# A two-layer decoder trunk on one core: modulation vectors by multiply-and-sum on VectorE instead of reductions on TensorE, layer-norm sums in column groups, and two small moves of TensorE's steps

## The chip, the cores and the metric

One NeuronCore of a Trainium2 chip (trn2) runs the whole program. The metric is the device time of one execution in microseconds (us); the median over several executions counts. All tensors are float32; "fp32r" in a row is the one-pass form of float32 on TensorE, for which every operand is split beforehand into a high and a low part.

## What is computed

From the reference, for depth 2, sequence 512 and D = 1024:

```python
e = silu(c @ cond_w + cond_b)
for i in range(2):
    mod = (e @ ada_w[i] + ada_b[i]).reshape(B, 3, 3, D)
    shift, scale, gate = mod[:, :, 0], mod[:, :, 1], 1 + mod[:, :, 2]
    h = modulate(x, norm_g[i, 0], shift[:, 0], scale[:, 0])
    x = x + 0.5 * gate[:, 0] * swiglu(h, ffn_w1[i, 0], ffn_w3[i, 0], ffn_w2[i, 0])
    h = modulate(x, norm_g[i, 1], shift[:, 1], scale[:, 1])
    x = x + gate[:, 1] * mixer(h)          # i = 0: causal conv module, i = 1: stick-breaking attention
    h = modulate(x, norm_g[i, 2], shift[:, 2], scale[:, 2])
    x = x + 0.5 * gate[:, 2] * swiglu(h, ffn_w1[i, 1], ffn_w3[i, 1], ffn_w2[i, 1])
# modulate(x, g, shift, scale) = rms_norm(x, g) * (1 + scale) + shift
# the conv module: glu(h @ w_in) -> depthwise conv of width 31 -> silu(layer_norm) -> @ w_out
```

## The kernel before

The kernel is written by hand, engine by engine, in raw instructions with semaphores; every engine runs its list in order. x lies transposed in the on-chip memory, 8 chunks of 128 channels by 512 tokens. There are four feed-forward parts (`ffn(j, ...)`, j = 0 to 3), the convolution module between j = 0 and 1 and the attention between j = 2 and 3.

**Slabs.** Weights come as slabs from HBM: up slabs of 128x2048 (22 per feed-forward part), down slabs of 128x1408 (16 per part). SyncE (SP) loads each into `raw[n % 2]`, ScalarE (ACT) writes its high part (`hi`, L630; in an up step L696), VectorE (DVE) its low part (`lo`, L896; in an up step L1103), and TensorE (PE) multiplies with three matmuls per product: high by high, high by low, low by high (`triple`, L1491 to L1493). An up slab is 48 matmuls of 128x512. The semaphore `lo_done` lets PE start a slab, and `slab_done` tells that it is finished. An up step of DVE (`up_step`) multiplies by SiLU's result (L1095), writes the low part of the activations (L1099), then the slab's low part (L1103).

**Modulation.** The 9216 values per layer are computed in groups of 512 (`q`; 38 groups in all, of which the first two are `cond_w`). Groups 0 to 5 are done on PE at the start (`start_group`, L1638, stages `stage[...]`). The other 32 are woven into the feed-forward parts 0 to 2: SP loads half a group (1 MB) into `ada_raw` (`load_ada`), DVE forms a weighted sum in eight instructions of 128x512 per group (`ada_half`, L905 and L908), PE sums it over the partitions in `ada_reduce` (L1619, four column groups of 32), which stands in the middle of an up slab (`at_k`) or behind a down slab, and DVE turns the row into columns and adds the bias (`ada_take`, L920, L922). `Q_FFN`, `Q_BODIES` and `Q_DOWN` say in which step which group is done.

**Norms.** For each modulated norm (number m; m = 2 is the layer norm) PE sums the squares in the first slab (`sums`, L1593), DVE computes the factor (`factor`) and writes it as two diagonals `fac_hi` and `fac_lo` (L964), and PE spreads these over the partitions (`spread`, L1611 and L1613) ahead of chunk 5 of the first slab, followed by `bias_sums` (L1571). Behind it `h_lows` on DVE and `h_his` on ACT make the modulated h, for which the second slab waits chunk by chunk (L1512, L1519).

**Layer norm (m = 2).** The mean is spread by L1747 and L1749; `token_sums` (L1716) forms per-token sums with 128-column weights and one moving column, four blocks per sum, for the sum and the sum of squares of v; earlier, `pivot` does the same for the first chunks (L1723, L1716). DVE centres the chunks (`centre`, L929), computes the factor (and writes it as diagonals, L970), PE spreads it, and then chunk by chunk DVE multiplies (L1304), ACT applies SiLU and writes `h_hi` (L784, L787), DVE writes `h_lo` (L1310), and PE does the first slab of the output projection.

**The start.** The groups' weights come in first. PE does groups 0 and 1 (the vector e), then group 2 (scale's first half), eight matmuls that keep PE busy (L1696), three chunks of the first slab, group 3 (scale's second half), and the other chunks; ACT makes the input's high parts (L659) and DVE the low parts (L995).

Of the kernel before, what the change touches and what calls it, by code (L numbers as in the profile page):

```python
# [22 lines left out]
ALU = mybir.AluOpType  # L23
# [63 lines left out]
Q_FFN = [6, 20, 31]  # L87
Q_BODIES = [11, 11, 7, 0]
Q_DOWN = 17
# [8 lines left out]
def trunk(nc, x_in, up_in, down_in, mix_in, ada_in, vec_in, dw_in, dwb_in, con_in, ind_in, sel_in, out):  # L98
    ctx = ExitStack()
    with ctx:  # L100
# [103 lines left out]
        ada_ps = ps[:, 7, 0:8]  # L204
        ada_rows = ps[:, 7, 0:P].rearrange("p (n r) -> p n r", n=4)
# [3 lines left out]
        ln_sq, ln_sum = ps[:, 4, 0:4], ps[:, 0, 0:4]  # L209
        pivot_ps = ps[:, 7, 0:4]  # L210
# [19 lines left out]
        ada_sum = sem("ada_sum")  # L230
        mod_done = sem("mod_done")
# [6 lines left out]
        lnsum_done = sem("lnsum_done")  # L238
        off_step = sem("off_step")
# [164 lines left out]
        def _(sp):  # L404
# [18 lines left out]

            def ffn_loads(j):
                nb = Q_BODIES[j]
                with sp.Fori(0, min(nb, 10)) if nb else ExitStack() as i:
                    if nb:
                        up_loads(j, i, True)
                if nb < 10:
                    with sp.Fori(nb, 10) as i:  # L430
                        up_loads(j, i, False)
                for s in range(2):
                    load(N_DOWN[j] + s, down_in[2 * KD * j + s, :, :], DOWN)
                    if nb == 11:
                        load_ada(2 * (Q_FFN[j] + 10) + s)
                for lo_i, hi_i in ((1, 2), (2, KD)) if j == 0 else ((1, KD),):
                    with sp.Fori(lo_i, hi_i) as i:
                        for s in range(2):
                            sp.wait_ge(lo_done, N_DOWN[j] + 2 * i - 1 + s)
                            sp.dma_start(raw[s][:, 0:DOWN], down_in[2 * KD * j + 2 * i + s, :, :]) \  # L440
                                .then_inc(raw_s[s], 16)
                        if j == 0 and lo_i == 2:
                            load_ada(2 * Q_DOWN - 2 + i)

# [24 lines left out]

            for c in range(2):  # L470
                load(N_CONV + c, mix_in[c, :, :])
# [152 lines left out]
        def _(act):  # L624
# [19 lines left out]
            def root(m):  # L644
                if m == 2:
                    act.wait_ge(vec_step, 4 * m + 1)
                    act.activation(st[:, 4:8], st[:, 0:4], ACT.Sqrt).then_inc(sqrt_done, 1)
                    return
                act.wait_ge(stat_col, stat_cols(m))
                act.activation(st[:, 4:8], row_cols, ACT.Sqrt, bias=eps_col, scale=1.0 / D) \  # L650
                    .then_inc(sqrt_done, 1)
# [80 lines left out]
            hi(N_UP[0])  # L732
            table()
# [158 lines left out]
        def _(dve):  # L892
# [6 lines left out]
            def ada_half(q, s, buf, acc):  # L899

                for k in range(4):
                    a = 8 * q + (STEP0 - 48) + 4 * s + k
                    w = e_col[:, 4 * s + k:4 * s + k + 1]
                    if s == 0 and k == 0:
                        dve.tensor_scalar(acc, buf[:, k, :], w, None, ALU.mult).then_inc(ada_step, 1)  # L905
                    else:
                        dve.wait_ge(ada_step, a)
                        dve.scalar_tensor_tensor(out=acc, in0=buf[:, k, :], scalar=w, in1=acc, op0=ALU.mult,  # L908
                                                 op1=ALU.add).then_inc(ada_step, 1)
# [22 lines left out]
            def factor(m):  # L932

                vv, sd, y0, y1 = st[:, 0:4], st[:, 4:8], st[:, 8:12], st[:, 16:20]
                if m == 2:
                    dve.wait_ge(stat_done, m + 1)
                    dve.wait_ge(off_step, 3)
                    dve.scalar_tensor_tensor(out=vv, in0=ln_sq, scalar=1.0 / D, in1=off_sq, op0=ALU.mult,
                                             op1=ALU.subtract).then_inc(vec_step, 1)
                    centre(2)  # L940
# [18 lines left out]
                for part in range(2):  # L959
# [3 lines left out]
                    if m != 2:  # L963
                        dve.tensor_tensor(  # L964
                            (fac_hi, fac_lo)[part].rearrange("p (b c i) -> p b c i", b=4, c=4),
                            ident[:, :].rearrange("p (b c i) -> p b c i", b=4, c=1).broadcast_to((P, 4, 4, 32)),
                            (f32(st_r[:, :]), y0)[part].rearrange("p (b c i) -> p b c i", b=1, i=1).broadcast_to((P, 4, 4, 32)),
                            ALU.mult).then_inc(rdiag_done, 1)
                        continue
                    dve.tensor_tensor(  # L970
                        (fac_hi, fac_lo)[part].rearrange("p (c m) -> p c m", c=4),
                        ident[:, :].rearrange("p (c m) -> p c m", c=1).broadcast_to((P, 4, P)),
# [1008 lines left out]
```

## Time and profile before

| | |
|---|---|
| three runs | 1976.23, 1976.68 and 1977.87 us; median 1976.68 us |
| the profiled execution | 1978.21 us, span 1976.4 us (1.8 us lie around it) |
| PE busy | 1945.8 us, 98% |
| DVE busy | 1110.3 us, 56% |
| ACT busy | 661.9 us, 33% |
| mean granted TensorE clock | 0.997 |
| HBM | 252 MB read, 129 GB/s over the span |

Busy time of PE is the union of its matmuls, whose ends are modelled. How much a step of PE costs is better read from the distance of matmul starts. The instruction count of a group with 32-bit float operands on PE that are not fp32r is twice the number of calls, since each call is two passes.

### The profile page before, as it was taken

The page shows a single profiled execution, that of the slowest core. Times are in us where ns is not written, and L with a number is a line of the kernel's source. Part 1 is how long each engine was busy: PE and PEld are TensorE (multiplying, and loading weights), DVE is VectorE, ACT ScalarE, POOL GpSimd, SP SyncE. Part 2 cuts the span into 40 slices and gives each one's busy share as a digit, 9 for nine tenths or more (in the row PEclk, how much of TensorE's full clock was granted, in tenths as well). Part 3 has the DMA queues.
Part 4 walks back from the last instruction along what each step waited for, and adds up shares of the span by engine and source line. Part 5 has one row for each costly group of instructions (what it writes and reads, how often), then busy time and mean ns, then how long its engine had stood idle before and what let it go on. Part 6 is the DMA issues. An engine that isn't in the chain of part 4 may idle for free.

```text
span 1976.4 us, 24087 instructions
## 1 busy us (share of the span) xinstructions
PE 1945.8 (98%) x9444; PEld 1562.6 (79%) x9444; DVE 1110.3 (56%) x1351; ACT 661.9 (33%) x742; POOL 150.5 (8%) x101
## 2 busy tenths in 40 slices
PE   6999999999989999999999999999999999999999
PEld 5788888876577888888888888888778788888887
DVE  4865564589888565633666533246569774333222
ACT  3422222242254322222432222234248743222211
POOL 0100000121411000001100000111022020000000
PEclk9999999999989999999999999999999999999999
DMA  9454544436413545432354522323245323222232
GB/s 394 170 206 176 206 165 166 158 106 180 126 55 138 208 174 194 175 124 93 116 213 170 191 93 79 102 100 124 95 99 137 107 86 107 85 106 85 88 98 90
DMA packets 50777, 275.88 MB, mean 140 GB/s; under 512 B 7456, under 2 KB 8096, under 8 KB 25760
## 3 DMA queue, kind: packets, MB, share of 16 engines
q1 hardware_dynamic: 47648, 270.87, 39.0%
q10 hardware_dynamic: 3072, 4.23, 0.9%
q8 instruction: 37, 0.61, 0.1%
q14 instruction: 20, 0.16, 0.0%
HBM read 251.94 MB, written 2.10 MB: 129 GB/s over the span
## 4 chain that ended last, share of the span: by engine, by line
PE 89%; DVE 4%; ACT 2%; issue 1%; DMA 0%; ACTq 0%; DVEq 0%; SPq 0%
PE ps L1491 27%; PE ps L1493 26%; PE ps L1492 26%; PE ps L1734 2%; PE ps L1512 1%; PE ps L1837 1%; PE ps L1853 1%; PE ps L1823 1%; PE ps L1619 1%; PE ps L1519 1%; DVE w L896 0%; PE ps L1532 0%; PE ps L1537 0%; PE ps L1531 0%; ACT h_hi L676 0%
## 5 line engine op out<-in xcount | busy, mean ns | idle before, releaser
L1491 PE MATMUL ps<-h_hi,w 128*128 128x512 f32 x1552 | 610.5, 393 | 1.2 <-DVE h_lo L995 1.0
L1493 PE MATMUL ps<-h_hi,w 128*128 128x512 f32 x1552 | 605.0, 390 | 0.0
L1492 PE MATMUL ps<-h_lo,w 128*128 128x512 f32 x1552 | 604.8, 390 | 0.0
L1491 PEld LDWEIGHTS ps<-h_hi,w 128*128 128x128 f32 x1552 | 291.7, 188 | 74.2 <-issue 12.8
L1493 PEld LDWEIGHTS ps<-h_hi,w 128*128 128x128 f32 x1552 | 291.5, 188 | 61.2
L1492 PEld LDWEIGHTS ps<-h_lo,w 128*128 128x128 f32 x1552 | 291.8, 188 | 58.8
L896 DVE TENSOR_TENSOR w<-raw,w 128x1408 fp32r<-128x1408 f32 (+1 forms) x104 | 201.0, 1933 | 204.4 <-ACT w L630 204.4
L630 ACT ACTIVATE w<-raw 128x1408 fp32r<-128x1408 f32 (+1 forms) x104 | 164.7, 1583 | 418.0 <-PE ps L1493 405.8
L1491 PE MATMUL ps<-g_hi,w 128*128 128x512 f32 x704 | 274.5, 390 | 0.0
L1493 PE MATMUL ps<-g_hi,w 128*128 128x512 f32 x704 | 274.2, 389 | 0.0
L1492 PE MATMUL ps<-g_lo,w 128*128 128x512 f32 x704 | 274.2, 389 | 0.0
L691 ACT ACTIVATE act_tmp<-ps 128x512 f32<-128x512 f32 x84 | 50.2, 597 | 551.0 <-PE ps L1493 539.9
L1103 DVE TENSOR_TENSOR w<-raw,w 128x2048 fp32r<-128x2048 f32 x76 | 174.2, 2292 | 74.3 <-ACT w L696 74.3
L1095 DVE TENSOR_TENSOR act_tmp<-act_tmp,ps 128x512 f32<-128x512 f32 x84 | 57.8, 688 | 256.0 <-ACT act_tmp L691 256.0
L908 DVE SCALAR_TENSOR_TENSOR ada_acc<-ada_raw,e_col,ada_acc 128x512 f32<-128x512 f32 x224 | 171.4, 765 | 6.8
L1491 PEld LDWEIGHTS ps<-g_hi,w 128*128 128x128 f32 x704 | 132.2, 188 | 27.7 <-issue 0.6
L1493 PEld LDWEIGHTS ps<-g_hi,w 128*128 128x128 f32 x704 | 132.3, 188 | 27.5
L1492 PEld LDWEIGHTS ps<-g_lo,w 128*128 128x128 f32 x704 | 132.3, 188 | 27.2
L696 ACT ACTIVATE w<-raw 128x2048 fp32r<-128x2048 f32 x76 | 144.5, 1901 | 0.0
L1076 DVE SCALAR_TENSOR_TENSOR x<-ps,gt,x 128x512 f32<-128x512 f32 x48 | 35.8, 749 | 131.6 <-PE ps L1493 131.6
L1099 DVE TENSOR_TENSOR g_lo<-act_tmp,g_hi 128x512 f32 (+1 forms) x84 | 58.1, 692 | 74.1 <-ACT g_hi L693 74.1
L693 ACT ACTIVATE g_hi<-act_tmp 128x512 f32 (+1 forms) x84 | 53.1, 632 | 82.9 <-DVE act_tmp L1095 82.9
(217 smaller groups left out, 1710.8 us busy)
## 6 DMA issues: line engine op xcount, KB each, us to landing
raw<-up_d SPq DMA_DIRECT2D x88, 1024.0 KB, 6.4
ada_raw<-ada_d SPq DMA_DIRECT2D x64, 1024.0 KB, 4.8
raw<-down_d SPq DMA_DIRECT2D x64, 704.0 KB, 4.1
raw<-mix_d SPq DMA_DIRECT2D x28, 1024.0 KB, 4.8
stage<-ada_d SPq DMA_DIRECT2D x12, 1024.0 KB, 20.1
stk<-parted SPq DMA_DIRECT2D x32, 256.0 KB, 4.0
stk<-parted SPq DMA_DIRECT2D x32, 128.0 KB, 2.3
u_blk<-u SPq DMA_DIRECT2D x48, 64.5 KB, 2.0
```

The lines of the kernel that those rows point to most:

```text
L630: act.activation(wsp[n % 2][:, 0, 0:cols], raw[n % 2][:, 0:cols], ACT.Copy).then_inc(hi_done, 1)
L691: act.activation(tmp, pair[s][0], ACT.Silu).then_inc(silu_done, 1)
L693: act.activation(g_hi[:, 2 * i + s, :], tmp, ACT.Copy).then_inc(ghi_done, 1)
L696: act.activation(wsp[s][:, 0, :], raw[s][:, :], ACT.Copy).then_inc(hi_done, 1)
L896: dve.tensor_tensor(wsp[n % 2][:, 1, 0:cols], raw[n % 2][:, 0:cols], f32(wsp[n % 2][:, 0, 0:cols]), ALU.subtract) \
L908: dve.scalar_tensor_tensor(out=acc, in0=buf[:, k, :], scalar=w, in1=acc, op0=ALU.mult, op1=ALU.add).then_inc(ada_step, 1)
L1095: dve.tensor_tensor(tmp, tmp, pair[s][1], ALU.mult).then_inc(g_full, 1)
L1099: dve.tensor_tensor(g_lo[:, 2 * i + s, :], tmp, f32(g_hi[:, 2 * i + s, :]), ALU.subtract).then_inc(g_done, 1)
L1103: dve.tensor_tensor(wsp[s][:, 1, :], raw[s][:, :], f32(wsp[s][:, 0, :]), ALU.subtract) \
L1491: pe.matmul(dst, a_hi_, b_hi_, start=start, stop=False, skip_group_check=True)
L1492: pe.matmul(dst, a_hi_, b_lo_, start=False, stop=False, skip_group_check=True)
L1493: return pe.matmul(dst, a_lo_, b_hi_, start=False, stop=stop, skip_group_check=True)
```

## The change

- **Modulation on VectorE.** The 32 later groups are no longer summed on PE. The weights come transposed (`mod_t`), in tiles of 128 outputs by 1024 inputs (512 KB), four per group, into `ada_tile`, one buffer that is the first half of the old one. DVE multiplies a tile by `e_row` (e, spread over all partitions) with a running sum into one column of `mods` (`ada_tile_sum`), and adds a group's four biases at once (`ada_bias`). `ada_half`, `ada_reduce` and their `ada_take` are gone. Tile loads stand between the slab loads of SP's list, one behind each tile sum.
- **Where.** `e_row` is made at the start: DVE writes e as diagonals (128x1024), PE spreads it with two float32 matmuls of 128x512 between groups 1 and 2, and ACT copies it from the two banks. Steps 0 of the three parts ("two slabs free of tiles") have none; parts 0 and 1 have ten steps with four tiles each, part 2 has nine; the down loop of part 0 has twelve tiles.
- **Layer norm and pivot.** `token_sums` uses 32-column weights of ones and 128 moving columns in four column groups, and DVE transposes the result. The order is: squares, sums, last squares. EPS is added on ACT and on DVE instead of beforehand. Fewer chunks are centred ahead of the loop (one before, one during and one after the factor, then c + 3 in step c). 11 matmuls on old data stand ahead of the spread and 8 behind it (`keep_clock`).
- **Start.** Group 3 moves from ahead of chunk 3 to ahead of chunk 2 of the first slab.
- **Spread.** In the norms other than m = 0 and m = 2, `fac_lo` is spread three matmuls behind `fac_hi`, and `bias_sums` behind it.

```diff
-Q_FFN = [6, 20, 31]
-Q_BODIES = [11, 11, 7, 0]
-Q_DOWN = 17
+Q_FFN = [5, 18, 28]
+Q_BODIES = [11, 11, 10, 0]
+Q_DOWN = 16
...
+            def ada_tile_sum(q, s, h):
+
+                dst = mods[:, :].rearrange("p (g n) -> p g n", n=4)[:, q - 2, 2 * s + h:2 * s + h + 1]
+                dve.wait_ge(ada_s, 64 * q + 16 * (2 * s + h + 1 - 24))
+                dve.scalar_tensor_tensor(out=ada_tile, in0=ada_tile, scalar=1.0, in1=e_row, op0=ALU.mult, op1=ALU.mult,
+                                         accum_out=dst).then_inc(ada_step, 1)
...
-                if between:
-                    between()
+                if ada:
+                    ada_tile_sum(Q_FFN[j] + i, s if turn is None else turn, 0)
                 dve.wait_ge(ghi_done, f + 1)
...
+                    ada_tile_sum(Q_FFN[j] + i, half, 1)
+                    if half == 1:
+                        ada_bias(Q_FFN[j] + i)
...
             def step_tiles(j, i, then_load, last=False):
                 for s in range(2):
+                    a = 4 * i + (TILE[j] + 2 * s)
+                    tile_load(a + 1)
+                    then_load(s)
+                    if not last or s == 0:
+                        tile_load(a + 2)
...
             for c in range(KD + 1):
...
-                if c + 5 < KD:
-                    centre(c + 5)
+                if c + 3 < KD:
+                    centre(c + 3)
...
-                    if k == 3 and m == 0:
+                    if k == 2 and m == 0:
                         start_group(3)
...
                     if k == 5 and m:
-                        spread(m)
-                        bias_sums(m)
+                        spread_part(m, 0)
...
                         last = triple(pair[0][b], w[:, 0, at], w[:, 1, at], hi_[:, k, :], lo_[:, k, :],
                                       k == 0, k == KD - 1)
+                        if k == 5 and b == 0 and m:
+                            spread_part(m, 1)
+                            bias_sums(m)
...
-            for n in range(3):
+            for n in range(2):
                 start_group(n)
+            pe.wait_ge(ediag_done, 1)
+            for b in range(2):
+                last = pe.matmul(pair[0][b], ones[:, :], ada_tile[:, S * b:S * b + S], start=True, stop=True)
+            last.then_inc(erow_sum, 1)
+            start_group(2)
             pe.wait_ge(lo_done, 1)
+            pe.wait_ge(erow_done, 2)
...
-                    last = pe.matmul(dst[:, b:b + 1], src[:, b * P:(b + 1) * P], ones[:, 0:1],
-                                     start=(start and b == 0), stop=stop, skip_group_check=True)
+                    last = pe.matmul(ps[32 * b:32 * b + 32, bank, 0:P], ones[:, 0:32], src[:, b * P:(b + 1) * P],
+                                     start=start, stop=stop, skip_group_check=True)
...
-            token_sums(ln_sum, v_sum, True, False)
-            token_sums(ln_sum, v[:, KD - 1, :], False, True).then_inc(lnsum_done, 1)
             pe.wait_ge(ss_step, ss_steps(2) + 6)
-            token_sums(ln_sq, ss, True, False)
+            token_sums(4, ss, True, False)
+            token_sums(0, v_sum, True, False)
+            token_sums(0, v[:, KD - 1, :], False, True).then_inc(lnsum_done, 1)
             pe.wait_ge(sq_done, KD * 2 + KD)
-            token_sums(ln_sq, prod[:, KD - 1, :], False, True).then_inc(stat_done, 1)
+            token_sums(4, prod[:, KD - 1, :], False, True).then_inc(stat_done, 1)
+            pe.wait_ge(lo_done, N_OUT + 1)
+            keep_clock(11)
             spread(2)
+            keep_clock(8)
```

The order of the instructions, at three places. First PE around the layer norm, before (L1734 are the convolution's taps, L1747 and L1749 the mean, L1716 the token sums, L1611 and L1613 the spread, L1512 the output projection):

```order
L1734 MATMUL ps<-u_blk,taps_w 32x512 x68
L1747 MATMUL ps<-v_sum,ones 128x512
L1749 MATMUL ps<-v,ones 128x512
L1716 MATMUL ps<-ones,v_sum 128x1 x4
L1716 MATMUL ps<-ones,v 128x1 x4
L1716 MATMUL ps<-ones,ss 128x1 x4
L1716 MATMUL ps<-ones,prod 128x1 x4
L1611 MATMUL ps<-parts,ones_r 128x512
L1613 MATMUL ps<-parts,ones_r 128x512
L1512 MATMUL ps<-h_hi,w 128x512 x4
```

and now:

```order
L1738 MATMUL ps<-ss,ones 32x128 x4
L1738 MATMUL ps<-v_sum,ones 32x128 x4
L1738 MATMUL ps<-v,ones 32x128 x4
L1738 MATMUL ps<-prod,ones 32x128 x4
L1745 MATMUL ps<-w 128x512 x11
L1642 MATMUL ps<-parts,ones_r 128x512 x2
L1745 MATMUL ps<-w 128x512 x8
L1541 MATMUL ps<-h_hi,w 128x512 x4
```

The sums have 128 moving columns instead of one, the squares come ahead of the sums, and the 19 matmuls of L1745 stand around the spread.

Second, DVE in the loop of up steps of part 0, one half of the loop's body, before:

```order
L1095 TENSOR_TENSOR act_tmp<-act_tmp,ps 128x512
L1099 ISA
L1099 TENSOR_TENSOR g_lo<-act_tmp,g_hi 128x512
L1102 REGISTER_ALU
L1103 TENSOR_TENSOR w<-raw,w 128x2048
L1111 ISA
L907 REGISTER_ALU
L908 SCALAR_TENSOR_TENSOR ada_acc<-ada_raw,e_col,ada_acc 128x512
```

and now:

```order
L1133 TENSOR_TENSOR act_tmp<-act_tmp,ps 128x512
L939 REGISTER_ALU
L940 ISA
L940 SCALAR_TENSOR_TENSOR ada_raw,mods<-ada_raw 128x1024
L1137 ISA
L1137 TENSOR_TENSOR g_lo<-act_tmp,g_hi 128x512
L1140 REGISTER_ALU
L1141 TENSOR_TENSOR w<-raw,w 128x2048
```

One tile sum (L940) stands ahead of the low part of the activations, the other behind the slab's low part; before, four instructions of 128x512 stood behind the latter (one is shown).

Third, PE in the first slab of a part, around the spread, now (L1520 to L1522 are the three matmuls of `triple`, L1642 the spread, L1602 `bias_sums`); before, L1611, L1613 and L1571 stood together ahead of these three:

```order
L1642 MATMUL ps<-parts,ones_r 128x512
L1520 MATMUL ps<-h_hi,w 128x512
L1521 MATMUL ps<-h_lo,w 128x512
L1522 MATMUL ps<-h_hi,w 128x512
L1642 MATMUL ps<-parts,ones_r 128x512
L1602 MATMUL ps<-ones,act_tmp 128x1 x2
```

The low part's spread and the bias sums have moved behind one product.

## Rows read from the trace of the kernel before

**Rows 1.** The page: each engine's busy time.

```profile
PE 1945.8 (98%) x9444; PEld 1562.6 (79%) x9444; DVE 1110.3 (56%) x1351; ACT 661.9 (33%) x742; POOL 150.5 (8%) x101
```

**Rows 2.** Timeline of PE, part 0 (start us, us, instruction, idle before it).

```profile
121.05 0.43 PE L1619 MATMUL ps<-ada_acc,ones 128*32 128x128 f32 x8
121.41 0.50 PE L1491 MATMUL ps<-h_hi,w 128*128 128x512 f32 x1
...
255.13 0.32 PE L1619 MATMUL ps<-ada_acc,ones 128*32 128x128 f32 x4
```

**Rows 3.** Timeline of PE, part 3, six pairs of slabs apart.

```profile
1690.17 0.39 PE L1491 MATMUL ps<-h_hi,w 128*128 128x512 f32 x1
...
1820.72 0.39 PE L1491 MATMUL ps<-h_hi,w 128*128 128x512 f32 x1
```

**Rows 4.** Groups by form of DVE (busy us, mean ns), whole run.

```profile
L1103 DVE TENSOR_TENSOR w<-raw,w 128x2048 fp32r<-128x2048 f32 x76 | 174.2, 2292 | 74.3 <-ACT w L696 74.3
L908 DVE SCALAR_TENSOR_TENSOR ada_acc<-ada_raw,e_col,ada_acc 128x512 f32<-128x512 f32 x224 | 171.4, 765 | 6.8
...
L1099 DVE TENSOR_TENSOR g_lo<-act_tmp,g_hi 128x512 f32 x72 | 49.8, 692 | 66.4 <-ACT g_hi L693 66.4
```

**Rows 5.** Timeline of ACT and DVE, one up step of part 1.

```profile
653.48 0.60 ACT L691 ACTIVATE act_tmp<-ps 128x512 f32<-128x512 f32 x1 [6.98 <-PE ps L1493]
...
657.39 2.29 DVE L1103 TENSOR_TENSOR w<-raw,w 128x2048 fp32r<-128x2048 f32 x1 [0.99 <-ACT w L696]
```

**Rows 6.** DMA issues: queue, count, KB each, median us to landing.

```profile
raw<-up_d SPq DMA_DIRECT2D x88, 1024.0 KB, 6.4
ada_raw<-ada_d SPq DMA_DIRECT2D x64, 1024.0 KB, 4.8
```

**Rows 7.** Timeline of PE's weight loads, part 1, start of the fourth slab.

```profile
630.73 0.19 PEld L1491 LDWEIGHTS ps<-h_hi,w 128*128 128x128 f32 x1 [0.53 <-DVE w L1103]
```

**Rows 8.** Timeline of PE, spread of norm m = 1.

```profile
415.55 0.39 PE L1611 MATMUL ps<-parts,ones_r 128*128 128x512 f32 x1
416.07 0.50 PE L1613 MATMUL ps<-parts,ones_r 128*128 128x512 f32 x1
```

**Rows 9.** Timeline of the pivot on PE, then of the layer norm, all engines.

```profile
503.27 1.02 PE L1723 MATMUL ps<-v_sum,ones 128*128 128x512 f32 x2
504.13 0.95 PE L1716 MATMUL ps<-ones,v_sum 128*128 128x1 f32 x8
504.94 0.48 PE L1491 MATMUL ps<-h_hi,w 128*128 128x512 f32 x1
...
546.16 0.69 DVE L970 TENSOR_TENSOR parts<-ident,st 128x512 fp32r<-128x512 f32 x1
...
547.97 0.68 DVE L1304 TENSOR_TENSOR act_tmp<-v,ps 128x512 f32<-128x512 f32 x1
...
550.30 1.19 PE L1512 MATMUL ps<-h_hi,w 128*128 128x512 f32 x2 [2.60 <-ACT h_hi L787]
...
560.00 0.63 ACT L787 ACTIVATE h_hi<-sq_tmp 128x512 fp32r<-128x512 f32 x1
...
563.27 0.39 PE L1491 MATMUL ps<-h_hi,w 128*128 128x512 f32 x1
```

**Rows 10.** Window: length, busy PE, PEld, DVE, ACT, POOL; PEclk, DMA, GB/s.

```profile
544.30:550.30 6.00, 1.59 (x2) 0.60 (x3) 5.79 (x15) 2.68 (x4) 0.00 (x0) 0.50 0.00 0
```

**Rows 11.** Timeline of the start: ACT, then PE.

```profile
17.58 0.19 ACT L731 ACTIVATE e_col<-e_pre 128x8 f32<-128x8 f32 x1
...
20.78 1.93 PE L1638 MATMUL ps<-stage,ada_acc 128*32 128x128 f32 x32 [4.15 <-DMA stage<-ada_d]
...
25.05 3.78 PE L1696 MATMUL ps<-w 128*128 128x512 f32 x8
28.63 0.52 PE L1491 MATMUL ps<-h_hi,w 128*128 128x512 f32 x1
...
37.51 0.47 PE L1491 MATMUL ps<-h_hi,w 128*128 128x512 f32 x1 [1.03 <-DVE h_lo L995]
```

More of the change, by code:

```diff
@@ L436, in ffn_loads @@
-                for lo_i, hi_i in ((1, 2), (2, KD)) if j == 0 else ((1, KD),):
-                    with sp.Fori(lo_i, hi_i) as i:
-                        for s in range(2):
[L439 to L443, printed above, removed]
+                up_load(j, 0, 0)
@@ new lines, in ffn_loads @@
+                up_load(j, 0, 1)
+                if j == 0:
+                    sp.wait_ge(erow_sum, 1)
+                    tile_load(0)
+                up_load(j, 1, 0)
+                up_load(j, 1, 1)
+                with sp.Fori(1, 9) as i:
+                    if nb:
+                        step_tiles(j, i, lambda s: up_load(j, i + 1, s))
+                    else:
+                        for s in range(2):
+                            up_load(j, i + 1, s)
+                for i in range(2):
+                    if i < nb - 9:
+                        step_tiles(j, 9 + i, lambda s: down_load(j, i, s), last=(nb == 10))
+                    else:
+                        for s in range(2):
+                            down_load(j, i, s)
@@ new lines, in ffn_loads @@
+                if j == 0:
+                    down_load(0, 2, 0)
+                    down_load(0, 2, 1)
+                    with sp.Fori(1, 6) as d:
+                        down_load(0, d + 2, 0)
+                        tile_load(2 * d + (TILE_DOWN - 1))
+                        down_load(0, d + 2, 1)
+                        tile_load(2 * d + TILE_DOWN)
+                    load(N_CONV, mix_in[0, :, :])
+                    tile_load(TILE_DOWN + 11)
+                    load(N_CONV + 1, mix_in[1, :, :])
+                    tile_load(TILE_DOWN + 12)
+                else:
+                    with sp.Fori(2, KD) as i:
+                        for s in range(2):
+                            down_load(j, i, s)
@@ L646, in root @@
                     act.wait_ge(vec_step, 4 * m + 1)
[L647 removed]
+                    act.activation(st[:, 4:8], st[:, 0:4], ACT.Sqrt, bias=eps_col).then_inc(sqrt_done, 1)
                     return
@@ L732, in _ @@
             hi(N_UP[0])
+            act.wait_ge(erow_sum, 1)
+            for b in range(2):
+                act.activation(e_row[:, S * b:S * b + S], pair[0][b], ACT.Copy).then_inc(erow_done, 1)
             table()
@@ L1077, in x_add, with up_step @@
                                          op0=ALU.mult, op1=ALU.add).then_inc(x_done, 1)
-            def up_step(j, i, s, ada, split=True, take=True, first=None, turn=None, between=None):
+            def up_step(j, i, s, ada, split=True, first=None, turn=None):
                 n = N_UP[j] + 2 * i + s
@@ L1129, in ffn @@
                     for s in range(2):
[L1130 to L1140 removed]
+                        up_step(j, 0, s, False, split=s > 0, first=FFN_ENTRY[j] if s == 0 else None)
+                with dve.Fori(1, 10) as i:
+                    for s in range(2):
+                        up_step(j, i, s, nb > 0)
                 for s in range(2):
```

193 lines of the change are left out of this document (82 added, 111 removed).

## The prediction

> **What bounds the kernel now.** I read the page first: PE is busy for 1945.8 of 1976.4 us, DVE for 1110.3 [rows 1]. PE stands idle for only 30.6 us in all, so time can come back from two places: work that leaves PE's list, and the few gaps in it. Then the timeline of PE, where the distance of two equal steps gives the true cost of what lies between them. In part 0 two reductions six pairs of slabs apart start at 121.05 and 255.13 [rows 2], 134.08 us, so 22.347 us for a pair with one reduction. In part 3, where none is left, six pairs take 1820.72 - 1690.17 = 130.55 us [rows 3], 21.758 us a pair. A pair is 96 matmuls, so one costs 0.227 us, and nothing but PE's own work fills either stretch. Last the gaps: the layer norm, where PE first multiplies again at 550.30 after an idle 2.60 us [rows 9], and at a granted clock of 0.50, that is 1.2 GHz, from 544.30 on [rows 10]; the start [rows 11]; and a short wait for a slab's low part in part 1 [rows 7].
>
> **Reductions off PE.** 22.347 - 21.758 = 0.59 us for each, of which the step itself takes 121.41 - 121.05 = 0.36 [rows 2] and the change to and from its form the rest. All 32 stand in stretches where PE is the bound, the four behind down slabs too: 32 x 0.587 = **18.8 us less**. Nothing on PE replaces them.
>
> **What DVE gets for it.** Per group the weighted sum was eight instructions of some 0.77 us [rows 4], plus the transposition. Now there are four tile sums of 128x1024. No row shows a sum with a running total. Between 0.69 us for 512 columns and 2.29 for 2048 [rows 4] a straight line gives 1.27 for 1024; the bounds are 1.2 and, if the total needs a second pass, 2.5. I take 1.27, since every float operation in these rows lies on that line. Per slab DVE then does 0.69 + 1.27 + 0.69 + 2.29 + 1.27 = 6.2 us of the 10.88 that PE needs. The first tile sum delays the activations' low part by 0.6 us or less, but the slab's low part waits for ACT anyway, 0.99 us in the row [rows 5]; it ends at 659.68, and PE wants it one slab of 10.88 us behind the slab's end, which released ACT at 653.48: not before 664.2. So the sums are hidden with 4.5 us to spare. That cover also holds for the tiles: with one buffer, the second tile of a step is loaded only behind the first sum. Issue to landing took 4.8 and 6.4 us for 1 MB [rows 6]; a tile is half of that, so 6.4 is the upper bound. Then DVE's cycle is 0.69 + 1.27 + 0.2 (SP's issue) + 6.4 + 1.27 = 9.8 us, under 10.88. SP's list is longer by 64 loads, but each slab load stands behind a tile load that is released earlier by the order on DVE, so slab loads are not held back; raw buffers have two slabs of time. Term: 0, with the condition kept for a rival.
>
> The Trainium skill (Vector Engine (DVE) Microarchitecture Reference, section 7, Points that are easy to get wrong) says that this instruction form with two float32 sources in the on-chip memory runs at half rate. By it a sum takes about 2.5 us; DVE's slab is then 8.7 us instead of 6.2 and the main sum unchanged, but the spare time for a tile's landing shrinks from 7.4 to 5.0 us. No row before shows such an instruction.
>
> **Steps 0 without tiles.** In parts 1 and 2 the fourth slab's weights wait 0.53 us for the low part [rows 7], because a half group of sums stands ahead of it on DVE. Those go, and the low part comes 2.7 us earlier: 0.47 us each (the step against one without the wait), **0.95** together. In part 0 the bias sums wait similarly for DVE, by about 0.25 us; with the switch of form **0.35**.
>
> **Spread.** The second spread starts 0.52 us behind the first [rows 8], where a matmul costs 0.227: a wait of 0.29 for the second diagonal. Three matmuls fill 0.68 us, so the wait goes: 5 norms x 0.29 = **1.45 less**. The spread row is complete some 0.4 us later, but DVE is then in a slab's low part of 2.29 us [rows 4], which covers it.
>
> **Pivot and layer norm.** The pivot's token sums take 504.94 - 504.13 = 0.81 us [rows 9], now 0.36 as in [rows 2]: 0.4 less, and everything behind is that much earlier; DVE's transposition (0.33 us) fits its 0.66 us of idle time ahead of the last chunk. In the norm, four sums of 0.9 us become four of 0.36. The last is complete 2.3 us earlier, the two transpositions and the added EPS cost DVE 0.7 again, so the factor comes 1.6 us earlier with the pivot's part in it, and the low diagonal (546.16 + 0.69 = 546.85 [rows 9]) at 545.2. DVE's first product started at 547.97, 1.12 behind it, with PE at 1.2 GHz; at 2.4 GHz this is about 0.6. So 545.9, 2.1 us earlier. Against that the loop has two more chunks to centre, 0.6 us each; DVE then sets the pace in five of eight chunks. Laying the steps out at their durations, the last high part ends at 559.3 (before 560.63 [rows 9]). PE needs 1.5 us behind it: 560.8 against 563.27 [rows 9], **2.4 less**. Before, PE trailed that part by 2.64 us because its first two chunks ran at half clock. The fillers lie in PE's waits: 11 x 0.227 = 2.5 us end at 543.6, ahead of the diagonal at 544.4; eight more end at 547.4, ahead of the first high part at 548.1. If they don't hold the clock, the eight take 3.4 us and the end is 561.3, so 2.0; bounds 1.2 and 3.3 (no cost of the loop).
>
> PE's clock was granted at 0.50 after its idle stretch [rows 10]. The Trainium skill (TensorE: Matmul & The Clock Gate, Part 1) gives the reduced clock as the state of an idle engine, which activity lifts; this trace agrees. By it the fillers keep 2.4 GHz, the 2.4 of the text above; without it 2.0.
>
> **The start.** e's columns are ready at 17.77 and DVE's diagonals (1.27) at 19.1 [rows 11, 4]. A float32 pass of 512 columns takes 0.86 / 2 = 0.43 us at full clock [rows 9]; the eight matmuls at 25.05 take 3.58 us [rows 11], 0.45 each, half the later pace. So the four passes take 3.4 us, until 22.5; group 2's first half could have begun at 20.78 [rows 11] and ends 1.25 us later with the second. The first slab begins between 0.3 later (the chain through DVE and ACT, if the clock rises earlier in the eight) and 1.1 later (if it does not). On the other hand group 3 comes one chunk, 1.36 us, earlier, which takes away the wait of 1.03 us at 37.51 [rows 11]: net 0.25 to 1.05, **0.7 less**; bounds 1.2 less, 0.6 more.
>
> **Sum.** 18.8 + 0.95 + 0.35 + 1.45 + 2.4 + 0.7 = 24.65 us. The profiled execution took 1978.21 us (span 1976.4 and 1.8 around it), 1.5 more than the median 1976.68; taken from the median, 1976.68 - 24.65 = **1952.0 us**, 1.2% less. About 0.2% (4 us) is what a measurement here can tell from no change.
>
> **Rivals.**
> (a) The reductions and small waits come back, but start and layer norm give nothing, since e's row costs its 1.25 us in full, the clock stays low and the fuller loop on DVE eats the earlier factor: 24.65 - 2.4 - 0.7 + 0.5 = 21 us less, 1955.6. For it: DVE's loop is in fact longer. Against: four sums get shorter by half a microsecond each on the path.
> (b) The reductions come back only in part, because DVE or a tile reaches PE now and then, most likely in the first steps of a part, where DVE is latest [rows 7]: 8 to 12 us less, about 1967. Against: 4.5 us to spare per slab.
> (c) **Slower**: the single tile buffer makes DVE the bound. The cycle 0.69 + 2x + 0.2 + L (x the sum, L the landing) passes 10.88 us if 2x + L is over 10.0. With x = 2.5 and L = 6.4 it is 12.3: 1.4 us for each of 58 steps is 81, less 4.5 of spare time in each of three parts (14) and less 24.65: 43 us slower, about 2019. It decides from L = 5.0 at that x. For it: the page's rule, and landings of 6.4 us. Against: those are of 1 MB, twice a tile.
> (d) The change does not do what it says, since the reductions' 0.59 us were DVE's or a loop's: no difference. Against: slab pairs of the other stretch are short by just this [rows 2, 3].
>
> **Chances.** Forecast 0.79, (a) 0.14, (b) 0.03, (c) 0.03, (d) 0.01. The range has to hold the forecast with its bounds (layer norm 3.3 and start 1.2: 1950.6; low ends 1.2 and -0.6: 1954.5) and (a): 1949.5 to 1957. Faster 0.96, same 0.01, slower 0.03.
>
> **What would show it.** No reduction in PE's list, and 21.76 us from pair to pair in part 0; a tile sum of 1.2 to 1.3 us (2.5 by the page) with DVE idle in each step; no wait at the fourth slab of parts 1 and 2; the two spreads 0.9 us apart with no idle time; a granted clock of 1.00 through the layer norm and the next full slab 2.4 us earlier counted from the taps' end plus 0.4; the first slab at 29 to 29.7 us with no wait ahead of chunk 4. I am wrong if the page shows PE waiting for low parts in the up steps, or pairs over 21.8 us.

## The result and the profile after

The changed kernel takes 1951.64 us (median of 4 executions, 1951.56 to 1952.25) against 1976.63 for the kernel before (4, 1976.23 to 1977.87): 25.0 us less, ratio 0.9873, 95% interval 0.9856 to 0.9890. The prediction was 1952.0. The profiled execution took 1952.25 us with a span of 1950.4. In the experiments one execution of `e12_before_fillers` took 3256.25 us at a mean granted clock of 0.557; it moves the median of its twelve by 0.04 us. The page, with the rows that answer to [rows 1], [rows 4] and [rows 6] (busy, mean ns; in the last three KB each and median us to landing):

```profile
PE 1923.8 (99%) x9211; PEld 1553.7 (80%) x9211; DVE 1075.6 (55%) x1323; ACT 663.4 (34%) x744; POOL 150.9 (8%) x101
...
L940 DVE SCALAR_TENSOR_TENSOR ada_raw<-ada_raw 128x1024 f32<-128x1024 f32 x128 | 163.3, 1276 | 96.1 <-DMA ada_raw<-mod_t_d 96.1
...
raw<-up_d SPq DMA_DIRECT2D x88, 1024.0 KB, 4.8
ada_raw<-mod_t_d SPq DMA_DIRECT2D x128, 512.0 KB, 4.0
```

PE is busy 22 us less, and its idle time falls from 30.6 to 26.6. The mean of a tile sum is 1.276 us, but no sum takes that: 122 of the 128 take 1.22 or 1.23 us, and six take 2.32. The straight line of the prediction gives 0.69 + (2.29 - 0.69) / 3 = 1.22 for 1024 columns, not the 1.27 that it names. VectorE sat idle for 96 us ahead of these sums, waiting for tiles; the prediction had counted one landing in each slab, and here both sums wait, as is shown below. Part 0, now, seen from VectorE: two products with SiLU's result, six pairs of slabs apart (timeline, the counterpart of [rows 2, 3]). Each is released by ACT, and ACT by PE, so they keep PE's pace:

```profile
103.88 0.69 DVE L1133 TENSOR_TENSOR act_tmp<-act_tmp,ps 128x512 f32<-128x512 f32 x1 [1.30 <-ACT act_tmp L725]
...
234.44 0.69 DVE L1133 TENSOR_TENSOR act_tmp<-act_tmp,ps 128x512 f32<-128x512 f32 x1 [2.36 <-ACT act_tmp L725]
```

130.56 us for six pairs, 21.76 each, as part 3 had all along [rows 3]. What PE waited for in the whole run (us in total, times, longest):

```profile
PE ps L1666 <- DMA stage<-ada_d: 10.4, 5, 7.1
PE ps L1712 <- DVE ada_raw L1211: 2.5, 1, 2.5
PE ps L1642 <- DVE parts L1008: 2.4, 4, 0.9
PE ps L1864 <- DVE sp_hi L1468: 2.1, 1, 2.1
PE ps L1843 <- ACT a_f L887: 2.0, 6, 0.3
PE ps L1520 <- DVE h_lo L1033: 1.1, 1, 1.1
PE ps L1761 <- DMA u_blk<-u: 0.7, 1, 0.7
PE ps L1666 <- DVE e_pre L961: 0.6, 1, 0.6
PE ps L1541 <- ACT h_hi L824: 0.5, 1, 0.5
```

No up step and no low part of a slab stands there. The layer norm had a wait of 2.60 us for ACT before [rows 9], and one for VectorE ahead of the spread (timeline of PE, before):

```profile
546.11 0.79 PE L1611 MATMUL ps<-parts,ones_r 128*128 128x512 f32 x1 [2.46 <-DVE parts L970]
```

Now (timeline of PE, then the window of six microseconds with PE's granted clock as third figure from the end, as in [rows 10]):

```profile
529.34 2.81 PE L1745 MATMUL ps<-w 128*128 128x512 f32 x11
533.07 0.50 PE L1642 MATMUL ps<-parts,ones_r 128*128 128x512 f32 x1 [0.91 <-DVE parts L1008]
533.87 0.50 PE L1642 MATMUL ps<-parts,ones_r 128*128 128x512 f32 x1 [0.30 <-DVE parts L1008]
534.20 2.01 PE L1745 MATMUL ps<-w 128*128 128x512 f32 x8
536.75 1.15 PE L1541 MATMUL ps<-h_hi,w 128*128 128x512 f32 x4 [0.54 <-ACT h_hi L824]
```

```profile
532.00:538.00 6.00, 4.25 (x17) 2.85 (x16) 5.90 (x13) 2.89 (x5) 0.00 (x0) 1.00 0.00 0
```

**Where the time went.** The trace lists every matmul, so the two profiles can be set against each other at the last matmul of each slab (us earlier than before, cumulative):

| up to | gain | of this step |
|---|---|---|
| end of the first slab (43.67 before) | 2.69 | start 2.7 |
| fourth slab of part 0 | 3.73 | bias sums 0.40, one reduction 0.59 |
| end of part 0 | 10.77 | 12 reductions, 0.587 each |
| second slab of the convolution | 11.36 | one reduction 0.59, spread 0 |
| last taps | 11.78 | pivot 0.31 |
| first slab behind the layer norm | 13.90 | layer norm 2.1 |
| end of part 1 | 20.39 | 10 reductions, fourth slab 0.47, spread 0.17 |
| end of part 2's up steps | 25.73 | 8 reductions, fourth slab 0.50, spread 0.15 |
| end | 26.00 | spread 0.17 and 0.16, small shifts |

The two profiled executions differ by 26.0 us, the medians by 25.0: the profiled one of before was 1.6 above its median. The experiments show which part of that was its start. Both profiles also hold a wait of 0.8 (before) and 0.7 us (now) for a DMA (`u_blk<-u`) ahead of the convolution's first taps; it nearly cancels between them.

### The profile page after: what moved, and what is told of

It reads as the page before. It is cut to its first block, busy times and chain, and to the rows that moved or that the text cites. A ratio compares the mean times of both kernels' runs of the same rounds, so it can differ in the third digit from the quotient of the medians.

```text
span 1950.4 us, 23638 instructions
## 1 busy us (share of the span) xinstructions
PE 1923.8 (99%) x9211; PEld 1553.7 (80%) x9211; DVE 1075.6 (55%) x1323; ACT 663.4 (34%) x744; POOL 150.9 (8%) x101
## 4 chain that ended last, share of the span: by engine, by line
PE 93%; DMA 2%; DVE 2%; ACT 1%; issue 1%; SPq 1%; ACTq 0%; POOL 0%; DVEq 0%
PE ps L1520 27%; PE ps L1521 27%; PE ps L1522 27%; PE ps L1761 2%; PE ps L1541 2%; DMA raw<-up_d 1%; PE ps L1548 1%; PE ps L1867 1%; PE ps L1883 1%; PE ps L1560 1%; PE ps L1561 1%; PE ps L1566 1%; PE ps L1853 1%; DMA stage<-ada_d 1%; SPq L492 0%
## 5 line engine op out<-in xcount | busy, mean ns | idle before, releaser
L1520 PE MATMUL ps<-h_hi,w 128*128 128x512 f32 x1552 | 606.0, 390 | 1.1 <-DVE h_lo L1033 1.1
L1522 PE MATMUL ps<-h_hi,w 128*128 128x512 f32 x1552 | 603.9, 389 | 0.0
L1520 PEld LDWEIGHTS ps<-h_hi,w 128*128 128x128 f32 x1552 | 291.3, 188 | 68.9 <-issue 7.9
L1522 PEld LDWEIGHTS ps<-h_hi,w 128*128 128x128 f32 x1552 | 291.3, 188 | 60.8
L1520 PE MATMUL ps<-g_hi,w 128*128 128x512 f32 x704 | 273.9, 389 | 0.0
L1522 PE MATMUL ps<-g_hi,w 128*128 128x512 f32 x704 | 273.9, 389 | 0.0
L940 DVE SCALAR_TENSOR_TENSOR ada_raw<-ada_raw 128x1024 f32<-128x1024 f32 x128 | 163.3, 1276 | 96.1 <-DMA ada_raw<-mod_t_d 96.1
L1522 PEld LDWEIGHTS ps<-g_hi,w 128*128 128x128 f32 x704 | 132.1, 188 | 27.5
L1520 PEld LDWEIGHTS ps<-g_hi,w 128*128 128x128 f32 x704 | 132.1, 188 | 27.4
L579 POOL TENSOR_TENSOR ss<-ss,sq_tmp 128x512 f32<-128x512 f32 x30 | 53.8, 1792 | 265.1 <-ACT sq_tmp L671 264.1
```

The lines of the kernel that those rows point to most:

```text
L579: pool.tensor_tensor(ss[:, :], a, sq_tmp[:, c % 2, :], ALU.add).then_inc(ss_step, 1)
L940: dve.scalar_tensor_tensor(out=ada_tile, in0=ada_tile, scalar=1.0, in1=e_row, op0=ALU.mult, op1=ALU.mult, accum_out=dst).then_inc(ada_step, 1)
L1520: pe.matmul(dst, a_hi_, b_hi_, start=start, stop=False, skip_group_check=True)
L1522: return pe.matmul(dst, a_lo_, b_hi_, start=False, stop=stop, skip_group_check=True)
```

## Experiments

Executions of one kernel scatter (23 of the kernel before: 1975.51 to 1977.62 us), and an interval of these ratios from four executions is 0.3% wide. So steps under 2 us are judged by their place in the profile as well. Stretches of it repeat to some 0.1 us where the clock is the same, with one exception: the wait ahead of the first taps is 0.7 to 0.9 us in the two first profiles, some 0.35 with group 3 moved in the kernel before, and absent in the others. The edits below are shortened, and remarks in brackets are not code.

**1. The reductions.** Is the 0.587 us PE's own?

```
+ def old_sums():
+     for b in range(4):
+         pe.matmul(ps[32*b:32*b+32, 6, 0:P], ones[:, 0:32], ones[:, :], ...)
```

> The changed kernel with 32 steps of four float32 matmuls of 32 columns (ones by ones, into a spare bank) put back on PE at the 32 places where the reductions stood; nothing reads them, and the tile sums on VectorE stay. If a reduction costs PE its 0.587 us by itself (the difference of slab pairs in the prediction), this gives back 18.8 us: 1951.6 + 18.8 = 1970.4. If the 0.587 us had come from VectorE's old work or its waits, and the new one removed it, less than 2 us: under 1953.6.

1970.97 us (10 executions, 1970.15 to 1972.14): 19.3 more than the change, 18.8 forecast. In the profile each of the 32 costs 0.59 again, while VectorE works as in the change. So they were PE's, and rival (d) is out. In the fourth slabs of the parts only these 0.59 come back, so the rest of their gain (0.40 to 0.50) is not the reductions'; no run takes it back by itself.

**2. The start.**

```
- if k == 2 and m == 0:
+ if k == 3 and m == 0:
      start_group(3)
```

> The changed kernel with the third start group behind chunk 2 of the first slab instead of behind chunk 1. If moving it is what freed the start (in the profile of before PE waited 1.03 us ahead of chunk 4, in the changed one not at all), the wait comes back at 1.0 to 1.1 us: 1952.7. If the start's gain (2.7 us in the profiles against a forecast of 0.7) is all the earlier rise of the granted clock, nothing changes: 1951.6. The profile also shows when the clock rises (13.28 us in the changed kernel's profile, 28.88 in that of before).

1952.86 (1952.73 to 1952.93), 1.2 more. The wait ahead of chunk 4 is back. The start of this run on PE:

```profile
18.05 3.78 PE L1712 MATMUL ps<-ada_raw,ones 128*128 128x512 f32 x4 [2.46 <-DVE ada_raw L1211]
...
24.72 2.14 PE L1718 MATMUL ps<-w 128*128 128x512 f32 x8
...
27.43 0.47 PE L1520 MATMUL ps<-h_hi,w 128*128 128x512 f32 x1 [0.58 <-DVE h_lo L1033]
...
36.28 0.47 PE L1520 MATMUL ps<-h_hi,w 128*128 128x512 f32 x1 [1.04 <-DVE h_lo L1033]
```

> The kernel before, unchanged, for a second profile of its start. In its first profile the granted clock rose at 28.88 us and the first slab ended (start of its last matmul) at 43.67; the changed start has shown 40.98 to 42.40 in five profiles whose clock rose at different moments. If the profiled execution of before was only late in its clock, this one's first slab ends up to 1.5 us earlier, and the true gain of the start is 1.2 to 2 us; if it ends at 43.7 again, the gain is the 2.7 us of the two profiles.

1976.34 us. Its first slab ended at 42.51, 1.2 earlier than in the first profile. PE in this second profile of the kernel before:

```profile
24.84 2.18 PE L1696 MATMUL ps<-w 128*128 128x512 f32 x8
27.53 0.47 PE L1491 MATMUL ps<-h_hi,w 128*128 128x512 f32 x1 [0.52 <-DVE h_lo L995]
```

In the first one the eight fillers ran at half pace, 3.78 us, and the slab began at 28.63 [rows 11]. Here they ran at full pace and it began at 27.53, as in the change (27.28 and 27.43): with e's row or without, PE waits for VectorE's low parts there. The clock's own moment was what differed.

> The kernel before with its third start group one chunk earlier in the first slab, as in the change, and nothing else of it. The two profiles of before put the first slab's end at 43.67 and 42.51 us with PE waiting 1.0 us ahead of chunk 4; undoing this part in the changed kernel cost 1.2 us. By that 1.2 us faster here too: 1975.2. If the start's gain needs the rest of the change, none: 1976.4.

The edit is the one above, the other way round, in the kernel before. 1975.41 (11 executions) against 1976.37 (23): 1.0 less; the ratio's interval, 0.9986 to 1.0004, does not exclude none. By the medians, moving the group alone is worth 1.0 to 1.2 us, the first of these within the noise. In its profile the first slab ends at 41.33, with no wait ahead of chunk 4.

**3. The layer norm.**

```
- keep_clock(11)
  spread(2)
- keep_clock(8)
```

> The changed kernel without the 19 filler matmuls of the layer norm. The prediction's step: PE's first chunks run at 1.2 GHz and the end comes 0.4 us later, since VectorE sets the pace in five of eight chunks: 1952.0. If instead the norm's gain is the clock's, the first slab behind it ends 2 us or more later: 1953.6 or above. If the clock does not fall without them, nothing: 1951.6.

1952.65 (1950.74 to 1953.36), 1.0 more. In its profile the first slab behind the norm ends 1.5 us later, counted from the last taps. PE and the window (clock 0.53 instead of 1.00):

```profile
532.67 1.50 PE L1642 MATMUL ps<-parts,ones_r 128*128 128x512 f32 x2 [3.74 <-DVE parts L1008]
536.55 2.05 PE L1541 MATMUL ps<-h_hi,w 128*128 128x512 f32 x4 [2.38 <-ACT h_hi L824]
538.40 1.05 PE L1548 MATMUL ps<-h_lo,w 128*128 128x512 f32 x2
539.25 1.91 PE L1541 MATMUL ps<-h_hi,w 128*128 128x512 f32 x4
```

```profile
532.00:538.00 6.00, 2.95 (x6) 1.76 (x7) 5.68 (x11) 2.85 (x5) 0.00 (x0) 0.53 0.00 0
```

A chunk of six matmuls takes 539.25 - 536.55 = 2.70 us there without a wait, while VectorE makes one in 1.8: at half clock PE is the bound of the first chunks.

> The kernel before with the 19 filler matmuls of the change ahead of and behind the layer norm's spread, its four short sums and its order on VectorE as they were. Leaving the fillers out of the changed kernel cost 1.5 us in the layer norm of its profile and 1.0 in the median; if the clock does the same here, 1.0 to 1.5 us faster, 1975.0, and the other 0.6 us of the norm belong to the sums and the earlier factor. By the prediction's step (0.4 us for the clock) 1976.1. The fillers need 2.5 us of a wait of 2.46; if they hold up the spread, slower by some 0.1.

Here the same two calls were added to the kernel before. 1975.30 (12 executions), 1.1 less, with an interval of 0.9987 to 1.0005. In the profiles the stretch from the end of the slab ahead of the last taps to the end of the first slab behind the norm takes:

| kernel | us | clock falls to 0.50 there for |
|---|---|---|
| before (and with group 3 moved) | 39.93, 41.19 (39.68) | 10.2 us, 13.7 us (10.2) |
| before with fillers | 38.83 | not |
| change without fillers | 39.32 | 10.2 us |
| change (and five kernels with the norm as it is) | 37.80 to 37.83 | not |

So a fall of 10.2 us costs about 1 us in the old norm (39.68 or 39.93 against 38.83) and 1.5 in the new one (39.32 against 37.81). The short sums with the earlier factor bring 1.0 at full clock (38.83 against 37.81) and 0.4 to 0.6 where the clock falls (39.32 against 39.68 and 39.93).

```
+ centre(1)             (ahead of the sums)
- centre(1)             (in the factor)
+ centre(2)
- centre(2)             (behind the factor)
+ centre(3), centre(4)
- if c + 3 < KD: centre(c + 3)
+ if c + 5 < KD: centre(c + 5)
```

> The changed kernel with the order of before in which VectorE centres the chunks of the layer norm: chunk 1 ahead of the sums, 3 and 4 behind the factor, so the loop has three to centre instead of five. In the changed kernel's profile VectorE is busy without a gap from 529.3 us to 544, so every instruction counts only once and the order alone decides when the row is asked for: the factor comes 0.6 to 0.7 us later, the loop is 1.2 us shorter. By the pace of VectorE the end is 0.5 us earlier or equal: 1951.1 to 1951.6. If the early factor is what the norm's 2.5 us rest on, 0.6 us or more later: 1952.2 or above.

1951.28 (1951.02 to 1951.67), and 37.93 us for the same stretch, 0.1 more. Neither the 0.5 earlier nor the 0.6 later of the expectation came: the order decides nothing. The likely reason is that VectorE has no gap there and only moves work from one side of the factor to the other.

**4. The spread.**

```
- if k == 5 and m: spread_part(m, 0)
+ if k == 5 and m: spread(m); bias_sums(m)
- (behind three products of chunk 5) spread_part(m, 1); bias_sums(m)
```

> The changed kernel with both spread matmuls and the bias sums together again ahead of chunk 5 in the first slab of norms 1, 3, 4, 5 and 6. The prediction's step (0.29 us of waiting for each) says 1.45 us slower, 1953.1. The comparison of the two profiles says something else: the first slab is 0.4 us shorter, and the second slab gives 0.2 (0.4 in norm 1) back, because its odd chunks' low parts are then awaited; by that 0.67 us slower, 1952.3. Under 0.3 us would say that the second slab takes it all.

1951.69 (1951.07 to 1952.30): no difference in the median, within the scatter. In the profile norms 3 to 6 each lose 0.16 to 0.18, norm 1 nothing: 0.7 us for all. Why it is less than 0.29 each is seen in the changed kernel, norm 3, in the second slab (PE, then GpSimd and PE's weight load, one row each):

```profile
599.88 1.07 PE L1541 MATMUL ps<-h_hi,w 128*128 128x512 f32 x4
600.78 0.61 PE L1548 MATMUL ps<-h_lo,w 128*128 128x512 f32 x2
601.24 1.07 PE L1541 MATMUL ps<-h_hi,w 128*128 128x512 f32 x4
602.23 0.73 PE L1548 MATMUL ps<-h_lo,w 128*128 128x512 f32 x2
```

```profile
600.87 1.31 POOL L585 TENSOR_TENSOR h_lo<-act_tmp,h_hi 128x512 fp32r<-128x512 f32 x1 [2.39 <-ACT h_hi L708]
...
602.23 0.30 PEld L1548 LDWEIGHTS ps<-h_lo,w 128*128 128x128 f32 x2 [0.34 <-POOL h_lo L585]
```

From a chunk's four high products to its two low ones it is 0.90 us in the first chunk here, 0.99 in the second, and its low ones then take longer too (0.73 against 0.61): PE now reaches the odd chunk's low part as GpSimd ends it (600.87 + 1.31 = 602.18). The first slab got shorter by 0.38, the second gives 0.2 back.

**5. The tile buffer.** VectorE's two sums in one slab of part 0 in the changed kernel (timeline of DVE; "idle before" in brackets):

```profile
161.14 1.23 DVE L940 SCALAR_TENSOR_TENSOR ada_raw<-ada_raw 128x1024 f32<-128x1024 f32 x1 [2.17 <-DMA ada_raw<-mod_t_d]
...
165.89 1.23 DVE L940 SCALAR_TENSOR_TENSOR ada_raw<-ada_raw 128x1024 f32<-128x1024 f32 x1 [0.71 <-DMA ada_raw<-mod_t_d]
...
169.16 0.69 DVE L1133 TENSOR_TENSOR act_tmp<-act_tmp,ps 128x512 f32<-128x512 f32 x1 [2.03 <-ACT act_tmp L725]
171.94 1.23 DVE L940 SCALAR_TENSOR_TENSOR ada_raw<-ada_raw 128x1024 f32<-128x1024 f32 x1 [2.10 <-DMA ada_raw<-mod_t_d]
```

Both sums of a slab wait for their tile. The one buffer is filled and emptied twice in 171.94 - 161.14 = 10.80 us here; single slabs scatter from 10.33 to 11.28, and the mean of eleven (118.53 to 236.69) is 10.74, under PE's 10.88 by 0.14. What does a slower sum do?

```
+ dve.scalar_tensor_tensor(out=ada_tile, in0=ada_tile, scalar=1.0, in1=e_row, ...)
  dve.scalar_tensor_tensor(out=ada_tile, in0=ada_tile, scalar=1.0, in1=e_row, ...)
```

> The changed kernel with each tile sum done twice by VectorE, in place (the products are multiplied by e again, so the modulation's numbers change; the work is otherwise the same). By the prediction's cycle (0.69 + 2 x 2.5 + 0.2 + one landing of 4.0 us = 9.9 us, under PE's 10.88) it costs nothing: 1951.6. By the loop that the changed kernel's profile shows (sum, landing 3.3, sum, landing 4.7 beside the slab's own load: 10.8 us for the two tiles of a slab) the tile buffer takes 13.2 us a slab and becomes the bound in 58 steps: 58 x 2.3 less 13 us of spare time is 120 us slower, about 2070; if both landings take 3.3 us, 12.0 us a slab and about 2005.

2019.88 us (2018.33 to 2021.69), ratio to before 1.0217 (1.0200 to 1.0234): 68 more than the change, and slower than the kernel before. VectorE, and what PE waits for:

```profile
160.51 1.22 DVE L941 SCALAR_TENSOR_TENSOR ada_raw<-ada_raw 128x1024 f32<-128x1024 f32 x1 [3.06 <-DMA ada_raw<-mod_t_d]
...
166.52 1.23 DVE L941 SCALAR_TENSOR_TENSOR ada_raw<-ada_raw 128x1024 f32<-128x1024 f32 x1 [0.70 <-DMA ada_raw<-mod_t_d]
...
172.66 1.23 DVE L941 SCALAR_TENSOR_TENSOR ada_raw<-ada_raw 128x1024 f32<-128x1024 f32 x1 [2.41 <-DMA ada_raw<-mod_t_d]
```

```profile
PE ps L1524 <- DVE w L1145: 39.9, 45, 1.2
...
PE ps L1524 <- DVE w L934: 7.6, 2, 3.8
```

The loop takes 12.15 us, and 58 x (12.15 - 10.88) = 74 us, less the spare time at each part's start, is about the loss (an estimate; 58 slabs have tiles). Both landings take 3.1 to 3.4 us in part 0's up steps, so of the expectation's two figures the second, 2005, had the landings nearly right, and came out too low. Part of the loss is the clock's: in each of the two waits of 3.8 us, at the second down slab of parts 0 and 1, the granted clock falls to 0.50 for 6.8 us, and there the run falls another 6.9 us behind the changed kernel. VectorE is busy only 61% of the whole span: its share of busy time did not show the bound, which is a loop of two sums and two landings.

> The changed kernel with only every second tile sum done twice (the odd tiles' numbers change by it). The loop of the tile buffer is two sums and two landings a slab. With every sum doubled the profile shows it alone: 12.15 us a slab (2 x (2.45 + 3.6)). Half the dose takes 1.23 us off: 10.9 us against PE's 10.88, if both landings stay at 3.2 us; then the time is within 3 us of the changed kernel, 1951 to 1955. If a landing falls beside the slab's own load (4.7 us, as in the changed kernel), the loop takes 12.4 us and the time is near that of the full dose: over 2000.

1951.38 (1951.31 to 1951.50): nothing, as the landings of the full dose say (12.15 - 1.23 = 10.92). In part 0's up steps of the changed kernel every second tile is issued some 2 us behind the slab's own load and takes 3.9 to 5.0 us to land; here it is issued some 3 us behind that load and takes 3.2 to 3.6. So 1.23 us more work in a slab lengthens the loop only from 10.74 to 10.89 us (mean of twelve slabs), which is PE's pace.

**6. GpSimd takes half of the norm's low parts; fillers in the attention.**

```
+ h_odds(2)             (GpSimd, behind its last distance)
- if c >= 1:
+ if c >= 1 and c % 2:  (VectorE's low parts of the layer norm, even chunks only)
```

> The changed kernel with the low parts of the layer norm's four odd chunks made by GpSimd, as in the other norms, instead of VectorE, which is the bound there (1.8 us a chunk from 534.4 to 544 us against PE's 1.36). It takes 4 x 0.6 = 2.4 us off VectorE; PE waited 450 + 540 + 530 + 385 less 4 x 250 ns = 0.9 us in the slab and 1.3 us ahead of it. If VectorE's pace is the whole of it: 0.9 to 1.5 us faster, 1950.4. If GpSimd's 1.3 us a part (or 2.2 us where VectorE reads two tensors from the same memory beside it) makes the odd chunks late, the same or up to 1 us slower.

1950.99 (1949.79 to 1952.08), which overlaps the executions of the change; the norm's stretch takes 37.24 us instead of 37.81. That is 0.6, under the 0.9 forecast: an odd chunk's low products now start as GpSimd's part ends (537.39 + 1.31 = 538.70; GpSimd, then PE):

```profile
537.39 1.31 POOL L585 TENSOR_TENSOR h_lo<-act_tmp,h_hi 128x512 fp32r<-128x512 f32 x1 [11.03 <-ACT h_hi L825]
```

```profile
538.75 0.73 PE L1551 MATMUL ps<-h_lo,w 128*128 128x512 f32 x2
```

```
+ if t == 1 and p == 0:
+     for _ in range(8): pe.matmul(ps[:, 6, :], con[:, 2, :], con[:, :, :], ...)
```

> The kernel with GpSimd's low parts in the layer norm (1950.99 us), and eight filler matmuls on TensorE where it waits 2.1 us for VectorE at the second head of the attention. In five of the nine profiles so far with this stage as it is the granted clock falls to 0.50 for 3.4 us right behind that wait, and the end is 1.1 us later than in the others. If the fillers keep it up: no fall in the profile, and 0.6 us faster in the median, 1950.4. If the fall has another cause: 1951.0.

1950.45 (1949.80 to 1950.99), and no fall in its one profile. (The count in the expectation should have been six of ten; in all thirteen profiles without these fillers it is nine.) The first window is of the changed kernel, behind that wait, with a clock of 0.72; the second is of this run, with 1.00:

```profile
1456.00:1462.00 6.00, 5.92 (x30) 5.27 (x29) 4.79 (x8) 4.36 (x7) 0.00 (x0) 0.72 0.75 175
```

```profile
1456.00:1462.00 6.00, 5.92 (x37) 5.18 (x37) 5.83 (x11) 5.42 (x9) 0.00 (x0) 1.00 0.54 130
```

As four of the thirteen profiles without these fillers show no fall either, the one of the run just above among them, one profile is no proof that they prevent it. Against that run the medians differ by 0.5 us, within its scatter; against the change by 1.2, with all four executions below the change's four.

## Why the prediction was right, and where its steps were not

- **Reductions**, 18.8: 0.587 each at 32 places in the two profiles, 19.3 by putting them back. Right.
- **Steps 0 without tiles**, 0.95 and 0.35: 0.97 and 0.40 in the two profiles. Right in size; no run tests the cause alone.
- **Spread**, 1.45: 0.65. The wait of 0.29 [rows 8] did go, but the step did not name what is late next: the second slab's odd low parts on GpSimd.
- **Pivot and layer norm**, 2.4: 0.31 and 2.1. The sum is right and its parts are not. "2.0 if the fillers don't hold the clock" put 0.4 on the clock, since VectorE sets the pace; it was 1.5 in the new norm. Of the 2.1, the sums and the factor brought 1.0 if the fillers are put in first (39.93, 38.83, 37.81), and 0.6 if they come last (39.93, 39.32, 37.81). VectorE's pace does not cover PE at half clock, as the chunk of 2.70 us shows.
- **Start**, 0.7 with a bound at 1.2: by the two profiles 2.7. Of this 1.2 is the late clock of the one profiled execution of before (43.67 against 42.51, and 42.40 in the kernel with fillers). Moving the group gave 1.0 to 1.2, and e's row cost nothing where 0.3 was charged, because the slab's start waits for VectorE in either kernel. So the first slab, forecast at 29 to 29.7 us, began at 27.28, and between 27.15 and 28.67 in nine profiles with this start. Against the mean of these three starts (42.86) the change's and those of eight more kernels with the same start (mean 41.23) gain 1.6. The one profile of before with the group moved ends the slab at 41.33, which would leave 0.1; by the medians some 0.5 of the 1.6 has no cause shown.
- **The sum**, 24.65 against 25.0: 0.8 too much for the spread and 0.9 too little for the start nearly cancel; that the forecast came within 0.4 us is luck in these two terms. The reductions, three quarters of the sum, are not luck. Rival (a)'s sum has a sign wrong: 24.65 - 2.4 - 0.7 + 0.5 is 22.05; its 21 us and 1955.6 follow from - 0.5.
- **Tiles, term 0**: right in the result, wrong in the working. "DVE's cycle is 0.69 + 1.27 + 0.2 + 6.4 + 1.27 = 9.8 us" counts one landing in a slab; two tiles through one buffer need two sums and two landings. That is 2 x (1.23 + 0.3 + 3.2) = 9.5 us if both land alone (an estimate; 0.3 lies between sum, issue, landing and sum), and 10.7 as measured, where one landing runs beside the slab's load. Rival (c) named the right loop and the wrong point of decision: with sums of 2.45 us the loop passes PE's slab from a landing of 2.6 us (2 x (2.45 + 0.4 + 2.6) = 10.9), not of 5.0. The doubled sums, at that very price, gave 2019.88 us where it had said 2019. That agreement is luck: its 12.3 us are two sums, one landing of 6.4 and a product, the 12.15 are two sums and two landings of 3.2. Its chance of 0.03 rested on the landing; what kept the change clear of it was the sum's 1.23 us.
- **The half rate** that the Trainium skill gives for this form (Vector Engine (DVE) Microarchitecture Reference, section 7, Points that are easy to get wrong) is not what 122 of 128 sums show: 1.22 to 1.23 us, the straight line's time. The other six are explained in the last section.

## What to carry to other kernels

Write the cycle of a single buffer as everything that happens to it between two equal moments, all its fills included; a fill that is behind other work is still in the loop, and an engine that is busy 61% of the time can be the bound through it. Where a wait goes, the next late thing takes a share: here half of what the spread gave in the first slab. Before a start or a norm is costed from one profile, take a second one of the same kernel: the clock's moment alone moved 1.2 us.

## What was not expected of the hardware

Six tile sums in part 0's down steps take 2.32 us instead of 1.23, and each runs beside GpSimd's sum of squares (timeline of DVE, then of POOL):

```profile
303.44 1.22 DVE L940 SCALAR_TENSOR_TENSOR ada_raw<-ada_raw 128x1024 f32<-128x1024 f32 x1
...
308.72 1.63 DVE L933 TENSOR_TENSOR w<-raw,w 128x1408 fp32r<-128x1408 f32 x1 [0.72 <-ACT w L664]
310.26 2.32 DVE L940 SCALAR_TENSOR_TENSOR ada_raw<-ada_raw 128x1024 f32<-128x1024 f32 x1
```

```profile
309.28 2.22 POOL L579 TENSOR_TENSOR ss<-sq_tmp 128x512 f32<-128x512 f32 x1 [251.34 <-ACT sq_tmp L671]
```

The two seem to take turns. GpSimd's instruction starts inside VectorE's low part, which ends undisturbed at 310.35, and takes 2.22 us; the same instruction takes 1.30 at 398.50, where VectorE had nothing under way as it began: 0.9 more, near the 1.07 that it overlaps. The tile sum, issued at 310.26 while GpSimd is still at work until 311.50, takes 1.09 more. In the kernel with doubled sums only the first of two is long (2.32, then 1.23). The Trainium skill (GPSIMD Engine Reference, section 1, Specifications) says that the two engines share their interfaces to the on-chip memory and contend where a VectorE instruction has two inputs there; these rows agree, and show that it is the later one that pays. And of the tile loop: half a dose more cost nothing, a full dose 68 us. A loop a hair under the bound does not tell how far it can be pushed, because the landings change with the moment of issue (3.9 to 5.0 us against 3.2 to 3.6).
